# One layer of a hybrid encoder in fp32: the order of the first quarters of the output projection

## The reference

```
y = jnp.concatenate([ya, yb, yc], axis=-1) @ w_out[l]
x = x + rms_norm(y, post_mix_g[l])
h = rms_norm(x, pre_mlp_g[l])
u = jnp.square(jax.nn.relu(h @ w_up[l])) @ w_down[l]
x = x + rms_norm(u, post_mlp_g[l])
```

## Time and profile before

| | us |
|---|---|
| time, median of 3 runs | 1326.0 (1325.99 to 1326.09) |
| the profiled execution's own time | 1326.84 |
| its span on the core | 1325.0 |
| PE busy with matmuls | 1293.4 (98%) |
| DVE busy | 814.7 (61%) |
| ACT busy | 647.1 (49%) |
| the 1216 matmuls of line 2179 with `w_hi` | 327.7 |

### The profile page before, as it was taken

One profiled execution on the slowest core, in us unless ns is written; L12 is line 12 of the kernel. 1 busy time (PEld: TensorE's weight loads), 2 busy tenths in 40 slices (PEclk: granted clock), 3 DMA queues, 4 the chain that ended last, 5 costly groups with the idle time before them and its releaser, 6 DMA issues.

```text
span 1325.0 us, 25435 instructions
## 1 busy us (share of the span) xinstructions
PE 1293.4 (98%) x10539; PEld 1137.8 (86%) x10539; DVE 814.7 (61%) x1134; ACT 647.1 (49%) x998; POOL 305.0 (23%) x255
## 2 busy tenths in 40 slices
PE   6999999999999999999999999999999999999997
PEld 5999988888899898888888888888888888888886
DVE  5556778787776977548555555555555555555565
ACT  5465564566434447447444444444444444444453
POOL 0011333234205221000555555555430000000000
PEclk9999999999999999999999999999999999999999
DMA  8656433333357345773866666666666666666672
GB/s 255 190 166 175 124 112 98 90 89 92 107 128 200 114 127 154 270 243 95 236 189 187 188 188 190 190 190 191 191 190 191 192 192 196 195 193 192 194 231 99
DMA packets 285895, 226.44 MB, mean 171 GB/s; under 512 B 15252, under 2 KB 263316, under 8 KB 284884
## 3 DMA queue, kind: packets, MB, share of 16 engines
q1 hardware_dynamic: 285312, 223.57, 57.4%
q0 software_dynamic: 240, 1.18, 0.3%
q10 hardware_dynamic: 228, 0.07, 0.0%
HBM read 222.69 MB, written 2.10 MB: 170 GB/s over the span
## 4 chain that ended last, share of the span: by engine, by line
PE 67%; DVE 3%; ACT 2%; issue 1%; DMA 1%; DVEq 0%; ACTq 0%
PE psum L2179 31%; PE psum L1798 18%; PE psum L1809 9%; PE psum L1782 2%; PE psum L1788 2%; PE psum L1783 2%; DMA raw<-in_w_out 1%; DVE w_lo L805 1%; ACT w_hi L1359 1%; PE psum L2155 0%; PE psum L2236 0%; DVE arena L1265 0%; PE psum L2057 0%; PE psum L2147 0%; PE psum L1944 0%
## 5 line engine op out<-in xcount | busy, mean ns | idle before, releaser
L805 DVE TENSOR_TENSOR w_lo<-raw,w_hi 128x1024 fp32r<-128x1024 f32 x394 | 497.0, 1264 | 389.1 <-ACT w_hi L1359 388.3
L1359 ACT ACTIVATE w_hi<-raw 128x1024 fp32r<-128x1024 f32 x394 | 418.7, 1066 | 444.8 <-PE psum L2179 186.7
L2179 PE MATMUL psum<-w_hi,act_both 128*128 128x512 f32 x1216 | 327.7, 389 | 1.5 <-DVE arena L1189 0.9
L2179 PEld LDWEIGHTS psum<-w_hi,act_both 128*128 128x128 f32 x1216 | 227.9, 188 | 49.9 <-issue 1.4
L1798 PE MATMUL psum<-act_both,w_hi 128*128 128x512 f32 x1024 | 247.0, 391 | 0.0
L1782 PE MATMUL psum<-act_both,w_hi 128*128 128x256 f32 x912 | 239.5, 296 | 1.8 <-issue 1.4
L1783 PE MATMUL psum<-act_both,w_hi 128*128 128x256 f32 x912 | 227.1, 283 | 0.0
L1798 PEld LDWEIGHTS psum<-act_both,w_hi 128*128 128x128 f32 x1024 | 188.1, 188 | 36.3
L2179 PE MATMUL psum<-w_lo,act_both 128*128 128x512 f32 x608 | 187.6, 389 | 0.0
L1782 PEld LDWEIGHTS psum<-act_both,w_hi 128*128 128x128 f32 x912 | 173.6, 190 | 10.2 <-issue 3.1
L1783 PEld LDWEIGHTS psum<-act_both,w_hi 128*128 128x128 f32 x912 | 174.2, 191 | 0.1
(11 more groups left out here) (237 smaller groups left out, 1056.0 us busy)
## 6 DMA issues: line engine op xcount, KB each, us to landing
raw<-in_w_up SPq DMA_DIRECT2D x128, 512.0 KB, 4.1
raw<-in_w_down SPq DMA_DIRECT2D x128, 512.0 KB, 4.4
raw<-in_w_in SPq DMA_DIRECT2D x114, 512.0 KB, 4.3
raw<-in_w_out SPq DMA_DIRECT2D x32, 512.0 KB, 4.8
arena<-in_x SPq DMA_DIRECT2D x2, 1024.0 KB, 6.1
arena<-in_na_rpb SPq DMA_DIRECT2D x16, 128.0 KB, 4.3
arena<-in_x SPq DMA_DIRECT2D x1, 2048.0 KB, 10.6
out_x<-arena SPq DMA_DIRECT2D x3, 512.0 KB, 2.7
```

The source lines that it names most:

```text
L805: dve.tensor_tensor(by_half(h, low(h)), by_pair(h, raw[:, place[h] % RAW]), by_half(h, high(h)).bitcast(F32), ALU.subtract).then_inc(s["lo ...
L1359: act.activation(by_half(h, high(h)), by_pair(h, raw[:, place[h] % RAW]), ACT.Copy).then_inc(s["hi_half"], 1)
L2179: last = pe.matmul(bank[4 * t + 2 * j + b], lhs[:, tokens], w[:, b * 512:(b + 1) * 512], start=start, stop=stop)
```

## The change

In the first depth, between the transposes `turn_o(2)` and the wait for `yf_ready` 3, the quarter (0,0) of the second depth is issued, with two waits ahead of it: for the low part of the second depth's activations (`y_lo` 2) and for the low part of its first half of weights (H2, `lo_half`). The second depth then has its own order for its three other quarters: (1,0) and `gemm_half`+1; wait for H3; (1,1), (0,1) and `gemm_half`+1. All the matmuls, their operands and banks are the ones of before, and the number of `gemm_half` counts is too.

```diff
                     part(n, lhs_hi, lhs_lo, 1, 0, True).then_inc(s["gemm_half"], 1)
                     pe.wait_ge(s["bank_free"], GROUPS)
                     turn_o(2)
+                    pe.wait_ge(s["y_lo"], 2)
+                    pe.wait_ge(s["lo_half"], place[2 * n + 2] + 1)
+                    part(n + 1, act_hi[:, OUT_ORDER[1]], act_lo[:, OUT_ORDER[1]], 0, 0)
                     pe.wait_ge(s["yf_ready"], RET_CT // 2)
                     part(n, lhs_hi, lhs_lo, 1, 1, True).then_inc(s["gemm_half"], 1)
+                    return
+                if n == OUT_H // 2 + 1:
+                    part(n, lhs_hi, lhs_lo, 1, 0).then_inc(s["gemm_half"], 1)
+                    pe.wait_ge(s["lo_half"], place[2 * n + 1] + 1)
+                    part(n, lhs_hi, lhs_lo, 1, 1)
+                    part(n, lhs_hi, lhs_lo, 0, 1).then_inc(s["gemm_half"], 1)
                     return
                 for j in range(2):
                     if j:
```

## The result

| | before | changed |
|---|---|---|
| time, median of 14 runs each on the same chips (us) | 1327.13 (1325.83 to 1329.83) | 1329.95 (1328.19 to 1331.09) |
| ratio | | 1.0020, 95% interval 1.0013 to 1.0027 |
| the profiled execution's own time (us) | 1326.84 | 1328.46 |
| its span (us) | 1325.0 | 1326.7 |
| mean granted clock in it | 0.999 | 0.998 |

The change makes the kernel about 2.8 us slower. The forecast was 1.24 us slower, at 1327.2 us, so the direction held and the size did not; the time lies outside the range given, 1326.4 to 1328.2 us. The kernel before, too, was slower in these 14 runs (1327.13) than in the three runs that the forecast started from (1326.0).

What follows compares the result with a forecast made beforehand. PE, busy 98% of the span, was taken to bound the kernel. A stall of 2.09 us in place of 0.85 adds 1.24 us, all else nothing: from the median 1326.0 to 1327.2 us, range 1326.4 to 1328.2.

Steps and rivals of the forecast that it cites:

- DVE's order holds PE, and PE begins at 521.62: At the transposes: `lo(H2)` stays behind `take_heads(2)`, so PE idles 2.09 us in place of 0.85, 1.24 us more.
- The 0.3 us that the prediction gave for `lo(H2)` ahead: At the transposes: were DVE free to pass, PE would begin near 520.7; cost 0.3 us instead of 1.24.
- The waits that hold already, and the slots: Behind the stall: satisfied waits cost 0 to 0.02 us each; later `hi(H4)` keeps 1.3 us of slack, no cost.
- Nothing behind gives the shift back: Wait for weights at 560.73 us: it shifts with PE and stays 0.6 us; 0 back, bounds 0 and 0.59.
- The clock: Behind the stall at the transposes: granted clock expected to stay at 1.00, nothing added to the sum.
- Rival (c): Behind the 2.09 us stall PE falls to 1.2 GHz, two quarters at half rate: 1329.9 us; chance 0.03.
- The base: Whole kernel before: the median of the runs shown, 1326.0 us, to which the difference was added.

Runs made afterwards that it cites:

- e_swap: The changed kernel with DVE's `lo(H2)` put ahead of `take_heads(2)`: 1328.32 us, ratio 1.0008.
- e_early: The changed kernel with H2's high and low part made in gaps of ACT and DVE ahead of the transposes: 1327.07 us, ratio 0.9997.
- the wait alone: The kernel before with only PE's wait for the low part of H2 put behind the transposes, no quarter moved: 1329.30 us, ratio 1.0014.
- the filled kernel: The changed kernel with four idle matmuls into free bank 6 in the stall behind `turn_o(2)`: 1328.13 us, ratio 1.0006.
- the two further profiles: The changed kernel, unaltered, profiled two more times to see the clock behind the stall: spans of 1328.6 and 1327.0 us.
- e_after: The changed kernel measured once more, nothing altered, against the kernel before: 1329.72 us, ratio 1.0017.
- the longer wait: The kernel before with PE's wait behind the transposes put for the low part of H3, no quarter moved: 1331.64 us, ratio 1.0030.

## Why the prediction was wrong, step by step

- *DVE's order holds PE, and PE begins at 521.62.* Right: 521.57 to 521.63 in the changed kernel's four profiles, a stall of 2.07 to 2.08 us for 2.09, 1.22 us more for 1.24. `e_swap` and `e_early` show the cause, since the stall goes to 1.19 us and to nothing when only the place of `lo(H2)` (and `hi(H2)`) changes. The 0.3 us that the prediction gave for `lo(H2)` ahead is borne out by this stall (1.19 - 0.85), not by the time.
- *The waits that hold already, and the slots.* Right: `hi(H4)` began at 524.65 for 524.73, no wait came at the third depth, and the wait alone costs as much as the whole change, within the intervals.
- *Nothing behind gives the shift back.* Right: the wait near 562 us did not shrink. It was taken as 0.6 us by its one profile, and it is a scattering quantity, 0.52 to 1.94 us over all profiles that have it there.
- *The clock.* This is the step that failed: a fall of the clock behind the stall was put at nothing in the sum. Rival (c) had the mechanism and the place, and was given 0.03. It was put aside on three grounds. The first was that the clock had stayed at 1.00 for 3.7 us behind PE's last matmul. The same stretch of the other profiles shows how far one such delay carries: from the end of the last matmul to the fall it is 2.1 to 5.0 us over the 17 profiles. The shortest is the one of the filled kernel shown above. The second was the full clock in all 40 slices of the page. That row can't show such a fall: a slice is 33 us long and its 9 stands for 90% or more, so half the clock for under 4 us, as in the stretches from 522 to 527 us above, leaves it at 9; it reads 9 throughout in all seven profiles that have a fall. The third was that 1.17 us of idle time had done nothing, which is so, but is a shorter stretch.
- *What the clock did in place of that.* The runs show a fall behind the 2.08 us in one of the changed kernel's four profiles, and a low mean clock in 15 of its 28 executions; a fall once behind 1.94 us, and in three of 13 profiles behind the 1.44 us at 18 us that the kernel before has as well. Whether it falls differs between executions of one kernel with the same timeline, so a single profile can neither show nor exclude it. The Trainium skill, "TensorE: Matmul & The Clock Gate", section "HAM oscillation — how this bites in real kernels", asks for a longer idle gap than this one before PE is throttled; the measurement decides, and a shorter one was enough.
- *The time of rival (c).* That its 1329.9 us meets the 1329.95 measured is luck. It took 2.7 us for a fall in every execution, on a base of 1326.0; the runs show 1.6 us for a fall (the two further profiles), in about half of the executions, on a base 1.1 us higher.
- *The sum with that term.* In the changed kernel's 28 executions 13 have a mean clock of 0.998 or more, at 1328.73 us on average, and 15 have 0.997, at 1330.46: 1.73 us for the fall, times 15/28, is 0.93. The kernel before has some of it too: 12 of 86 executions, 1.32 us above its others, which is 0.18. So the change adds 0.75. With 1.22 for the stall and 0.4 for the wait near 562 us, which isn't shown to be the change's, that is 2.37 us; the means lie 2.60 apart in the first measurement (1329.66 and 1327.06) and 2.27 in `e_after` (1329.66 and 1327.39). The median moves by 2.8 because more than half of the executions are in the upper group.
- *The base.* The three runs that I started from all lay near 1326.0, the low end of what the kernel before does (1325.8 to 1330.5 us in later runs). The range was made 1.8 us wide on them; 1.1 us of the miss is this alone.

## What to carry to other kernels

Before work is put into an idle stretch, look where each of its inputs stands in its producer's list: here the moved quarter needed the instruction right behind the one that PE was already waiting for, and the stall more than doubled, from 0.85 to 2.07 us. In a kernel like this one, price an idle stretch of PE of two microseconds not at its length alone but with a chance of the lower clock behind it: here that took about half of the executions, and cost those 1.7 us where the longer stall cost 1.22. If the stretch can't be avoided, fill it with a few matmuls into a free bank whose result nobody uses; four of them took that part away here. A single profile of a kernel whose times scatter by 3 us is one draw: read its own time against the list of times first.

## What the runs showed of the hardware

The fall of the clock is not tied to the idle stretch in a fixed way. In one execution of the changed kernel the granted clock was still 1.00 when PE came back at 521.6 us and fell to 0.50 at about 522.9, under full work; with the longer wait it fell at the same 522.9 us with PE still idle; behind the last matmul it held for 2.1 to 5.0 us of idle time. Two executions with PE timelines equal to 0.03 us up to the stall went either way. Each fall cost 1.6 to 1.7 us at the transposes and at 562 us, and 1.4 to 1.5 us near 20 us. In the profiles whose chain of waits runs through it, the transfer of weights behind the 3 MB of `x` and `gains` took 11.98 to 13.33 us, and a burst cut into pieces moved the wait (562 to 582 us) and did not remove it.
